# Two transformer blocks on one Trainium2 core: input projection, forget-gate attention, latent projections and latent attention joined into one program

## The reference, cut to what matters

```python
def hybrid_mixer(h, positions, w_in, q_norm_g, w_uq, kv_norm_g, w_ukv, b_forget, w_o_mla, w_o_fox, w_out):
    cq, ckv, k_rope, fq, fk, fv, f_logit, g_mla, g_fox = jnp.split(h @ w_in, IN_OFFSETS, axis=-1)
    q = (rmsnorm(cq, q_norm_g) @ w_uq).reshape(b, s, 8, 64 + 32)
    kv = (rmsnorm(ckv, kv_norm_g) @ w_ukv).reshape(b, s, 8, 64 + 64)
    q_rope, k_rope = rope(q[..., 64:], positions), rope(k_rope, positions)
    o_mla = causal_block_attention(q_mla, k_mla, v_mla, MLA_SCALE)
    f_cum = jnp.cumsum(log_sigmoid(f_logit + b_forget), axis=1)
    o_fox = causal_block_attention(fq, fk, fv, FOX_SCALE, f_cum)
    y = sigmoid(g_mla) * (o_mla @ w_o_mla) + sigmoid(g_fox) * (o_fox @ w_o_fox)
    return y @ w_out
```

## Time and profile before

| what | value |
| --- | --- |
| median of three runs | 3186.43 us (3180.01 to 3188.55) |
| the profiled execution, its own time | 3183.08 us |
| its span, first to last instruction | 3181.3 us |
| TensorE busy | 2988.7 us, 94% of the span |
| VectorE, ScalarE, GpSimd busy | 1594.8, 800.9, 1040.0 us |
| mean granted TensorE clock | 0.965 of full speed |

### The profile page before, as it was taken

How to read it: one execution, slowest core, us unless ns; L and a number is a source line. 1 busy time by engine, 2 the same in 40 slices (tenths; PEclk the granted TensorE clock), 3 DMA queues, 4 the chain that set the end, 5 groups by cost and what they waited for, 6 DMA issues and landing times. The chain is left out here.

```text
span 3181.3 us, 34450 instructions
## 1 busy us (share of the span) xinstructions
PE 2988.7 (94%) x13294; PEld 2373.0 (75%) x13294; DVE 1594.8 (50%) x1598; ACT 800.9 (25%) x1072; POOL 1040.0 (33%) x468
## 2 busy tenths in 40 slices
PE   6999998999999999989999696799998999999998
PEld 5876576788888886768887563577786888888886
DVE  3639955545555566741210566645546433334356
ACT  2138942211121122220011244133203211111112
POOL 2330032444444442424433311410243343343342
PEclk9999999999999999999999698879999999999999
DMA  2121031123222322121132330200331111111112
GB/s 105 49 71 27 1 146 47 53 80 98 100 92 94 104 86 93 46 101 46 54 107 97 86 80 27 66 14 14 127 112 33 53 47 53 46 46 51 48 46 73
DMA packets 69594, 216.38 MB, mean 68 GB/s; under 512 B 9088, under 2 KB 15488, under 8 KB 68736
## 3 DMA queue, kind: packets, MB, share of 16 engines
q1 hardware_dynamic: 65616, 200.48, 20.0%
q10 hardware_dynamic: 3888, 14.68, 1.1%
HBM read 170.50 MB, written 22.54 MB: 61 GB/s over the span
## 5 line engine op out<-in xcount | busy, mean ns | idle before, releaser
L278 POOL TENSOR_TENSOR w_hi<-w_raw,inv_count 128x1024 fp32r<-128x1024 f32 x194 | 373.2, 1924 | 1689.5 <-PE ps L316 1098.1
L281 POOL TENSOR_TENSOR w_lo<-w_raw,w_hi 128x1024 fp32r<-128x1024 f32 x194 | 512.7, 2643 | 15.3
L316 PE MATMUL ps<-x_hi,w_hi 128*128 128x512 f32 x1216 | 378.1, 392 | 16.0 <-POOL w_lo L281 10.0
L316 PE MATMUL ps<-x_lo,w_hi 128*128 128x512 f32 x1216 | 376.7, 391 | 0.0
L316 PE MATMUL ps<-x_hi,w_lo 128*128 128x512 f32 x1216 | 376.4, 391 | 0.0
L316 PEld LDWEIGHTS ps<-x_hi,w_hi 128*128 128x128 f32 x1216 | 230.1, 190 | 65.7 <-issue 11.9
L316 PEld LDWEIGHTS ps<-x_lo,w_hi 128*128 128x128 f32 x1216 | 229.7, 189 | 48.3
L316 PEld LDWEIGHTS ps<-x_hi,w_lo 128*128 128x128 f32 x1216 | 229.7, 189 | 48.0
L316 PE MATMUL ps<-hidden_hi,w_lo 128*128 128x512 f32 x800 | 246.3, 389 | 0.0
L316 PE MATMUL ps<-hidden_lo,w_hi 128*128 128x512 f32 x800 | 246.3, 389 | 0.0
L316 PE MATMUL ps<-hidden_hi,w_hi 128*128 128x512 f32 x800 | 246.3, 389 | 0.0
(11 more groups left out here) (401 smaller groups left out, 5085.4 us busy)
## 6 DMA issues: line engine op xcount, KB each, us to landing
w_raw<-wall SPq DMA_DIRECT2D x221, 512.0 KB, 3.6
ada_raw<-wada SPq DMA_DIRECT2D x48, 512.0 KB, 4.3
gates_scratch<-gate_out ACTq DMA_DIRECT2D x16, 512.0 KB, 2.6
gate_in<-gates_scratch SPq DMA_DIRECT2D x8, 1024.0 KB, 7.9
residual<-x_t SPq DMA_DIRECT2D x8, 512.0 KB, 8.7
residual<-x_t SPq DMA_DIRECT2D x2, 2048.0 KB, 9.8
emb_scratch<-emb_out ACTq DMA_DIRECT2D x8, 512.0 KB, 2.6
embedding<-emb_scratch SPq DMA_DIRECT2D x2, 2048.0 KB, 11.9
```

The source lines that it names most:

```text
L278: nc.gpsimd.tensor_tensor(w_hi[:, slot, :], w_raw[:, slot, :], one.to_broadcast([P, S]), ALU.mult).then_inc(w_split, 1)
L281: nc.gpsimd.tensor_tensor(w_lo[:, slot, :], w_raw[:, slot, :], w_hi[:, slot, :].bitcast(F32), ALU.subtract).then_inc(w_split, 1)
L316: last = nc.tensor.matmul(ps[:, banks + c, :], lhs, x[:, k0 + k, c * HALF:(c + 1) * HALF], start=(left == nk * 3 - 1), stop=(left == 0))
```

## The change

The four Blocks from fox to the output side become stages of one program with everything before them (`fox_*`, `proj_*` beside `mla_*`), and there is no meeting of the engines between in2 and the end. What stood at the start of fox, proj and mla moves ahead:

- The fox values are no longer transposed. Four weight loads bring a quarter of the rows of all four value blocks each, and TensorE multiplies with tokens as the stationary side, 192 matmuls of 512 columns as before. VectorE and ScalarE copy four tiles each. mla's values are made in the same way from one weight block.
- Squares, sums, reciprocal roots, scaling and splitting of the latents run during in2, beside tiles 2 to 9. The ten split tiles (5.2 MB) go to an HBM scratch and come back during fox, after score 36 of 48, with the rotation table.
- The rotated key rows, the forget gates and the split of fox's first pair run on ScalarE and VectorE between the 16 gate blocks; SP issues the 28 DMAs of the first fox pair between the weight loads of the last gate blocks.
- The order of proj is now keys, values, queries. It takes four bank pairs in turn. Head pair 0 of the mla queries is split within it, and the key tiles of pair 0 are filled there.
- Later stages get other slots, and the bank pairs of mla and of the output projection are rotated by one.

```diff
--- before.py
+++ after.py
...
+    def fox_move(sp, p, half, h):
+        (q_h, q_l), (k_h, k_l) = ((t[:, 0, :], t[:, 1, :]) for t in (later_split if p else first_split))
+        b = p % 2
+        cs = slice(half * HALF, (half + 1) * HALF)
+        r = slice(h * HD, (h + 1) * HD)
+        for src, dst, at in ((k_h, k_both, 0), (k_h, k_both, HD), (k_l, k_rest, 0),
+                             (q_h, q_both, 0), (q_l, q_both, HD), (q_h, q_rest, 0)):
+            sp.dma_start(dst[b][at:at + HD, h, cs].bitcast(F32), src[r, cs].bitcast(F32)
+                         ).then_inc(moved[b][half].sem, 16)
...
     def in2_sync(sp):
         load_blocks(sp, GI + 3, GI + 4)
         sp.wait_ge(*residual_ready.at(0))
...
-        load_blocks(sp, GI + 4, GI + 37)
+        load_blocks(sp, GI + 4, GI + 5)
+        sp.dma_start(mask_in[:, :], consts[:, 5 * P:6 * P]).then_inc(mask_landed.sem, 16)
+        load_blocks(sp, GI + 5, GI + 31)
+        sp.wait_ge(*kq_split.at(4))
+        for half in range(2):
+            for h in range(2):
+                fox_move(sp, 0, half, h)
+                load_blocks(sp, GI + 31 + 2 * half + h, GI + 32 + 2 * half + h)
+        fox_rows(sp, 0)
+        load_blocks(sp, GI + 35, GI + 37)
 
     def in2_pool(pool):
         split_low(pool, GI + 1)
-        split_blocks(pool, GI + 2, GI + 35)
+        split_blocks(pool, GI + 2, GQ + 1)
...
+            if t < 7:
+                act.wait_ge(*v_full.at(t + 1))
+            else:
+                wait_tile(act, GI + FV + 3, 1, 0, 0)
+            nc.scalar.activation(v_tok2[:, t, :], ps[:, V_BANK[t], :], ACT.Identity).then_inc(v_rest.sem, 1)
+        for g in range(5):
+            gate(g)
...
+        gate(5)
+        act.wait_ge(*rope_done.at(3))
+        nc.scalar.activation(rope_hi[R_ROWS, 0, :], rope_k[R_ROWS, 0, :], ACT.Identity).then_inc(rope_split.sem, 1)
...
+        gate(6)
+        gate(7)
+        act.wait_ge(*f_step.at(5))
+        for t, k in zip(first_split, (FQ, FK)):
+            nc.scalar.activation(t[:, 0, :], raw2[:, k, :], ACT.Copy).then_inc(first_hi.sem, 1)
+        for g in range(8, N_GATES):
+            gate(g)
...
+        def latent_stat(n, total, banks, added):
+            pe.wait_ge(*square_added.at(added))
+            for c in range(2):
+                last = nc.tensor.matmul(ps[:, banks + c, :], neg_ones_f, total[:, 0, half(c)], start=True, stop=True)
+            last.then_inc(stat_full.sem, 1)
         next_two(pe, GI, x_hi, x_lo, {3: stat_1})
-        dense(pe, GI + 2, 32, 8, 1, x_hi, x_lo, job0=2)
+        dense(pe, GI + 2, 4, 8, 1, x_hi, x_lo, job0=2)
+        pe.wait_ge(*rstd_ready.at(4))
+        latent_stat(0, msq, 4, 3)
+        dense(pe, GI + 6, 2, 8, 1, x_hi, x_lo, job0=6)
+        latent_stat(1, msq_kv, 6, 5)
+        dense(pe, GI + 8, 6, 8, 1, x_hi, x_lo, job0=8)
+        for i in range(4):
+            b = GI + FV + i
+            pe.wait_ge(w_split, b * 2 + 2)
+            for t in range(8):
...
+                for kk in range(2):
+                    k = 2 * i + kk
+                    for n, (x, w) in enumerate(((x_hi, w_hi), (x_hi, w_lo), (x_lo, w_hi))):
+                        wv = w[:, b % 2, :].rearrange("p (m k c) -> p k m c", m=4, k=2)[:, kk, :, :]
+                        last = nc.tensor.matmul(
+                            ps[:, V_BANK[t], :].rearrange("p (m c) -> p m c", m=4), x[:, k, ts], wv,
+                            start=k == 0 and n == 0, stop=k == 7 and n == 2)
...
+        def gate(b, slot, u, job):
+            pe.wait_ge(w_split, b * 2 + 2)
+            pe.wait_ge(*pair_free.at(job - 1))
+            product(pe, slot, 0, 8, x_hi, x_lo, 0, 4 + 2 * u).then_inc(w_used, 1)
+        for u in range(2):
+            pe.wait_ge(*v_first.at(2 * u + 2))
+            gate(GI + 18 + u, (GI + u) % 2, u, 14 + u)
...
-            for m in range(4):
-                for b in range(8):
-                    last = nc.tensor.transpose(ps[:, 2 * m + b // 4, (b % 4) * P:(b % 4 + 1) * P],
-                                               raw2[:, FV + m, b * P:(b + 1) * P], ident_f)
-                last.then_inc(turn_full.sem, 1)
-            pe.wait_ge(*evac.at(4))
-            pe.wait_ge(*mask_set.at(1))
-            fox.tensor(pe)
...
+    def fox_sync(sp):
+        for p in range(1, 4):
+            sp.wait_ge(*kq_split.at(4 * p + 4))
+            if p >= 2:
+                sp.wait_ge(*score_full.at(12 * (p - 1)))
+            for half in range(2):
+                for h in range(2):
+                    fox_move(sp, p, half, h)
...
+        sp.wait_ge(*score_full.at(36))
+        for t, first, count in lat_at:
+            sp.dma_start(t[:, :, :].bitcast(F32), lat_dram[first:first + count, :, :].rearrange("m p n -> p m n")
+                         ).then_inc(lat_in.sem, 16)
+        sp.wait_ge(*moved[1][0].at(512))
+        sp.dma_start(rope[:, :, :], rope_dram).then_inc(lat_in.sem, 16)
+
+    def fox_pool(pool):
+        pool.wait_ge(w_used, GQ + 2)
+        pool.wait_ge(*krope_stored.at(0))
+        nc.gpsimd.memset(fox.negs[:, :, :].bitcast(F32), 1.0).then_inc(set_rows.sem, 1)
...
+            if p == 1:
+                pool.wait_ge(*kq_split.at(8))
+                split_blocks(pool, GQ + 1, GQ + 2)
...
+    def fox_tensor(pe):
+        pe.wait_ge(*v_first.at(0))
+        pe.wait_ge(*mask_set.at(0))
+        fox.tensor(pe)
...
+    def proj_sync(sp):
+        load_blocks(sp, GQ + 3, GQ + 4)
+        sp.wait_ge(*score_full.at(0))
+        rope_rows(sp, 0)
+        load_blocks(sp, GQ + 4, GQ + 5)
+        key_rows(sp, 0)
+        load_blocks(sp, GQ + 5, GQ + 9)
+
+    def proj_pool(pool):
...
+        pool.wait_ge(*set_rows.at(2))
+        split_blocks(pool, GQ + 3, GQ + 7)
+
+    def proj_scalar(act):
...
+    def proj_tensor(pe):
+        def entry(n):
+            if n < 3:
+                with before(FOX):
+                    pe.wait_ge(*consumed(JOBS[last_job(proj_pair(n))]))
+            elif n == 3:
+                pe.wait_ge(*o_free.at(0))
+            pe.wait_ge(*pair_free.at(n - 3))
+
+        def tile(n, slot, at, ks):
+            entry(n)
...
+        pe.wait_ge(w_split, GQ * 2 + 2)
+        pe.wait_ge(*lat_in.at(96))
+        for m in range(4):
+            tile(m, GQ % 2, 2 * m, (3, 4)).then_inc(tile_full.sem if m < 3 else w_used, 1)
...
+        for h in range(8):
+            n = 8 + h
+            wait_proj(dve, n)
+            dve.wait_ge(*pair_free.at(n))
+            nc.vector.tensor_tensor(qm[h][rows, :], pair(proj_pair(n))[rows, :], rope_cos[rows, 0, :], ALU.mult
...
+            nc.vector.tensor_tensor(r_a[rows, 0, :], pair(proj_pair(n))[swap, :], rope_sin[swap, 0, :], ALU.mult
+                                    ).then_inc(pair_free.sem, 1)
+            dve.wait_ge(*pair_free.at(n + 1))
+            dve.wait_ge(*dve_step.at(2 * h + 1))
+            nc.vector.tensor_tensor(qm[h][rows, :], qm[h][rows, :], r_a[rows, 0, :], ALU.add
...
+            if h >= 2 and h < 4:
+                for half in range(2):
+                    q_low(dve, 0, h - 2, half)
+    PROJ = ((lat_in, 96), (act_step, 9), (dve_step, 16), (tile_full, 10), (pair_free, 16))
...
+                                      pe.wait_ge(*q_split.at(4 * p + 2 * c + 2 if p else 4)),
+                                      pe.wait_ge(*set_rows.at(5 if p else 2))),
...
```

More of the change, by code:

```diff
@@ new lines, in in2_vector @@
+        V = nc.vector
+        for b in range(4):
+            copy(b)
+        for n in range(3):
+            add_square(n)
+        copy(4)
+        copy(5)
+        for n in range(3, 5):
+            add_square(n)
+        dve.wait_ge(*mask_landed.at(16))
+        V.tensor_copy(mask[:, :], mask_in[:, :]).then_inc(mask_set.sem, 1)
+        dve.wait_ge(*cols_in.at(16))
+        copy(6)
+        dve.wait_ge(*rstd_ready.at(6))
+        for n in range(3):
+            latent(n)
+        copy(7)
@@ new lines, in in2_vector @@
+        for n in range(3):
+            latent_low(n)
+        copy(8)
+        dve.wait_ge(*rstd_ready.at(8))
+        for n in range(3, 5):
+            latent(n)
+        copy(9)
+        for n in range(3, 5):
+            latent_low(n)
+        for b in range(10, 14):
+            copy(b)
+        V.tensor_scalar(raw2[fr, KRF, :], raw2[fr, KRF, :], cols[fr, COLS2["b_forget"]:COLS2["b_forget"] + 1], None,
+                        ALU.add).then_inc(f_step.sem, 1)
+        dve.wait_ge(*lat_stored.at(32))
@@ L2014, in __init__, with bank @@
             self.max_ready, self.row_out, self.o_out = max_ready, row_out, o_out
+            self.turn, self.entry = turn, entry
+        def bank(self, kind, n):
+            return 2 * ((JOB_NO[kind, n] + self.turn) % 3)
         def p_at(self, k, cs=None):
@@ L2354, in _program @@
-    rope = slots("rope", 14, 2)
+                    lambda p: raw2[:, FQ + p, :],
+                    lambda pe, m: pe.wait_ge(*(pair_free.at(-1) if m == 2 else v_rest.at(0))))
+    lat_at = [(22, 0, 4), (14, 4, 1), (26, 5, 2), (15, 7, 1), (32, 8, 2)]
+    cx = {}
```

(27 more changed lines are left out.)

717 lines of the change are left out of this document (351 added, 366 removed).

## The result

The changed kernel takes 3103.25 us (median of 4 runs, 3100.84 to 3104.94) beside 3187.42 us before in the same runs; the ratio is 0.9745 with the 95% interval 0.9733 to 0.9757. It is faster by some 84 us where I had forecast 110, and it lies 5 us above my range (3062 to 3098).

The account below looks back on a forecast made before the run. TensorE was taken to set the pace, with three preparation gaps followed by half clock. Terms summed to 268.6 instead of 378.9 us, a gain of 110.3 from 3183.08: 3072.8, plus 3.35 for the median, 3076; range 3062 to 3098.

Parts of the forecast that it names:

- In2: Stage before fox: two added sums over partitions cost 3.8 us, value products and moved-in work nothing.
- Pairs 1 to 3 of fox: Fox after its first pair: length stays as before, 99.9 us.
- projections: Between fox and mla: 240 matmuls at 0.226 take 54.3 us against 68.5, with four bank pairs in turn.
- The three gaps: TensorE's near-idle 26.5 us before fox and 30.4 before projections go to 0; 17.3 before mla gives way to its entry.
- 13.38 and 17.44 us of work: TensorE work at half clock in fox's and mla's entries, to take half as long at full clock.
- a stall: Fox pair 0: TensorE waits 2.8 to 4.1 us, taken as 3.3, for pair 1's operands.
- rival B: Clock drops at mla's entry: work after the lag +6.9 us, pair 0 55.2 (+10.0), total 3093; chance 0.17.
- Entry of mla: To mla's first exponential: VectorE ends 10.3 us behind TensorE, then 8.3; 18.6 us instead of 36.2.
- Rival C: Mla's entry: GpSimd blocks VectorE longer on heads 6, 7 and six maxima, 1.5 to 8 us; 3080; chance 0.1.
- Entry of fox: Fox's start: first maxima, row copy and score at 6.7 us plus 1.4 for ScalarE; 8.1 instead of 16.3.
- Fox pair 0: Fox's first pair: 35.4 us plus a wait of 3.3 for pair 1's operands, 38.7 us.
- Mla pair 0: Mla's first pair: 45.2 us, the middle of 43.9 and 46.5, instead of 55.2.

Follow-up runs that it names:

- e1: Changed kernel with twelve further TensorE products at fox's entry, six ahead of the first negated maxima and six ahead of the row copy; 3096.81 us.
- e2: Changed kernel with filler products at mla's entry, ahead of the first three maxima, the first negated maxima and the row copy; 3089.64 us.
- e12: Changed kernel, its order of projections kept, with filler products at both entries and ahead of later negated maxima in fox and mla; 3087.79 us, ratio 0.9707.
- e3: Changed kernel with a GpSimd weight split, two memsets and pair 1's key split held until VectorE has turned mla's eight heads; 3095.84 us.
- e8: e1 and e4 combined, without fillers ahead of fox's first negated maxima, GpSimd's splits in both first pairs held until after negated maxima; 3088.99 us.
- e4: Changed kernel with projections ordered keys, queries, values instead of keys, values, queries; 3079.25 us in one execution, 3089.49 to 3091.67 us in five later runs.

## Why the prediction was wrong

*Right.* In2: fox began at 1751.4 instead of 1747.3, +4.1 for my +3.8; that the two are so close is luck, since other traces with the same instructions up to there begin fox up to 4.6 us later. No gap before fox, none before the projections, latents in time. Pairs 1 to 3 of fox 99.7 us (99.9), projections 54.8 (54.3), no wait for sums of squares. What lies behind mla's pair 0 took as long as before (1055.0 for 1055.1 us of the span). The three gaps were worth what I said. The sign, the end of the three gaps and VectorE as the next one to be late were right.

*The step that failed* was the assumption that full clock comes back once the gaps are gone. I halved 13.38 and 17.44 us of work, took pair 0 of fox at 35.4 without half clock (plus a stall) and that of mla at 45.2, and wrote that the low level came only behind gaps. In the changed kernel it also came in the entries: behind two waits of 1.5 us in a row (fox), and in mla within the second of four waits, one of 2.68 us that followed one of 0.96. Once down, it stayed for 23.9 and 51.2 us. e1, e2 and e12 show that it goes when the waits are filled. This was my rival B, which I had for mla alone, at 0.17, and priced at 16.9; by e12 it cost some 12 there and 5 in fox. Its argument against, that the waits are short with work between them, is what the runs refute. Its 3093 lacked the same loss in fox and the sizes below.

I had also misread a row. I wrote that half clock stood behind each gap, but the projections ran at 0.99 right behind theirs of 30.4 us, and kept full clock through waits for VectorE as long as 2.7 us. Trace of the kernel before, the stretch behind the first 0.9 us and the longest of these waits:

```profile
1967.20:2034.80 67.60, 60.50 (x273) 47.84 (x271) 54.81 (x41) 12.29 (x12) 22.99 (x10) 1.00 0.13 39
1978.24 0.73 PE L316 MATMUL ps<-latent_hi,w_hi 128*128 128x512 f32 x2 [2.73 <-DVE rope_a L2417]
```

Between the waits stand products of 512 columns there, and products of 128 to 512 columns with their masks in the two entries. The gap or wait alone does not set the clock; what stands around it counts too. Which property of it does, no run isolates.

The Trainium skill, "TensorE: Matmul & The Clock Gate", Part 1, says that activity releases the lower level. I had kept the row's price against that, and for the pair the row was right: in the changed kernel mla's pair 0 took 55.2 us again, at 0.77 on average with TensorE 97% busy.

*Sizes.* Full clock apart, by e12 against my terms:

- Entry of mla 25.4 for 18.6. VectorE ended its heads 15.1 us behind TensorE for my 10.3. I costed four query splits at the 2.5 us that the earlier trace rows gave; there GpSimd only filled memory beside them, here it split weights and they took 8.4. Heads and splits took 43.6 us (1932.47 to 1976.04) for my 38.7. e3 shows that GpSimd is the reason. Rival C had this mechanism and nearly this size, 4 us for 5, but the size was luck, since C had the wrong place. It put the loss on heads 6 and 7 and the six maxima, and the instructions of these two heads took 1.22 us as ever. The loss lay in the query splits beside GpSimd's weight splits; the heads' third instructions took less than before, 14.4 for 15.9 us. The other 2 us of the entry are VectorE's scaling of eight columns, 2.18 us in e12 beside GpSimd's key split.
- Entry of fox 10.3 for 8.1, from the first maximum: VectorE's scaling of eight columns took 1.54 us beside GpSimd's split (0.17 in the pair's second half), and TensorE waits for it 1.53. I had this in neither entry. e8, with the split held, had 8.9 from there.
- Fox pair 0 39.9 for 38.7. The size is nearly right and the reason wrong: pair 1's operands caused no wait. SP had its last short rows out at 1774.8, they take 1.7 us to land, and at full clock they would be wanted at 1776.9 (14.1 behind the first exponential at 1762.8); the longer entry had covered them. At full clock the place is taken by 3.8 us for VectorE's negated maxima (e1).
- Mla pair 0 46.2 for 45.2.

The Trainium skill, "SBUF — State Buffer", section "Who interferes with whom", says that an instruction of VectorE with two SBUF inputs contends with a GpSimd instruction that reads SBUF, and that the shared ports are an exclusive lock. I let the row of before decide the sum against it. The changed kernel's trace agrees with the page instruction by instruction: a third instruction of a head that starts inside a split takes 2.4 to 3.0 us and one outside 1.22; the one of 2.98 us ends 1.07 us behind the split's end, the one of 2.96 us 1.09, so nearly all of it came after. The one that started 0.16 us ahead of a split took 1.22, and that split 2.81 instead of 1.89: here the first to start kept its time. What the average of the earlier trace rows hid is how many instructions meet a split, and that is a question of the schedule.

## What to carry to other kernels

Do not take the clock as given once a gap is closed: look at what TensorE does at the start of the stage behind it, and if short products alternate with waits for VectorE and ScalarE, give half clock in the next pair a price and a real chance, or put products into the waits, which here gave 5 us (e1) and 12 us (e2) in one execution each, and together 12 by the ratios and 15 by the medians of four executions (e12). When a wait in front of a stage goes, everything that was prepared in it (splits on GpSimd above all) moves beside VectorE's work; cost VectorE's instructions with two SBUF operands by those that had such company, not by their mean. One execution that owes 12 us to the clock at a single place, as e4 did, has to be run again before its edit is credited with them.
